# Expert mixture of a two-layer diffusion backbone: experts in pairs, latent rows in two partition halves, context rows in native fp32

## The reference, cut to what matters

```python
D_MODEL, SEQ, CTX_LEN, DEPTH = 1024, 512, 256, 2
N_EXPERTS, EXPERT_FF, CAPACITY_FACTOR = 16, 1024, 2

def _expert_choice_ffn(h, w_router, w1, w3, w2):
    B, T, D = h.shape
    cap = CAPACITY_FACTOR * T // N_EXPERTS
    aff = jax.nn.softmax((h @ w_router).astype(jnp.float32), axis=-1)
    vals, idx = lax.top_k(aff.transpose(0, 2, 1), cap)
    xg = jax.vmap(lambda hb, ib: hb[ib])(h, idx)
    hid = jax.nn.silu(jnp.einsum('becd,edf->becf', xg, w1)) * jnp.einsum('becd,edf->becf', xg, w3)
    y = jnp.einsum('becf,efd->becd', hid, w2) * vals[..., None].astype(h.dtype)
    return jax.vmap(lambda yb, ib: jnp.zeros((T, D), h.dtype).at[ib.reshape(-1)].add(yb.reshape(-1, D)))(y, idx)

# in each layer l: latent stream always, context stream in layer 0 only, with the same weights
ml = _expert_choice_ffn(hl, w_router[l], w_exp_gate[l], w_exp_up[l], w_exp_down[l])
xl = _layer_norm(alpha * xl + g2 * ml, ln2_g[l], ln2_b[l])
```

## Time and profile before

| | |
|---|---|
| median of 3 runs | 3953.68 us (3949.96 to 3955.05) |
| the profiled execution | 3951.19 us, span 3949.5 us |
| busy: PE, weight loads, DVE, ACT, POOL | 3482.3, 2718.0, 2316.6, 1588.2, 779.9 us |
| expert stage of layer 0, of layer 1 | about 1467 to 2168 us, 3255 to 3912 us of the span |
| weight matmuls of the experts (L1228) | 4608 |
| scatter matmuls (L835, 96 rows) | 680 |
| adds to acc (L2042) | 340 |
| mean granted TensorE clock | 0.942 of 2.4 GHz |

### The profile page before, as it was taken

One profiled execution on the slowest core, in us unless ns is written; L12 is line 12 of the kernel. 1 busy time (PEld: TensorE's weight loads), 2 busy tenths in 40 slices (PEclk: granted clock), 3 DMA queues, 4 the chain that ended last, 5 costly groups with the idle time before them and its releaser, 6 DMA issues.

```text
span 3949.5 us, 50430 instructions
## 1 busy us (share of the span) xinstructions
PE 3482.3 (88%) x19426; PEld 2718.0 (69%) x19426; DVE 2316.6 (59%) x3472; ACT 1588.2 (40%) x2055; POOL 779.9 (20%) x467
## 2 busy tenths in 40 slices
PE   5998898889999869999998199898899969999994
PEld 3997677878887746666665189578766756666663
DVE  2594741501111649998997674742322359999996
ACT  3113742411110226666664322754211126666662
POOL 2001013121110113323322200112222112222231
PEclk7999999999999989999998599999999979999997
DMA  6131123031112359888897122131122219999994
GB/s 236 66 128 59 44 97 118 17 107 39 58 64 76 109 184 308 311 309 306 309 311 268 60 75 75 49 97 43 40 94 96 90 61 317 324 327 327 328 331 150
DMA packets 331412, 632.85 MB, mean 160 GB/s; under 512 B 14142, under 2 KB 104398, under 8 KB 324846
## 3 DMA queue, kind: packets, MB, share of 16 engines
q1 hardware_dynamic: 309056, 557.88, 40.7%
q0 software_dynamic: 22192, 72.68, 5.6%
HBM read 614.00 MB, written 16.50 MB: 160 GB/s over the span
## 4 chain that ended last, share of the span: by engine, by line
PE 65%; DVE 11%; issue 9%; ACT 6%; DMA 5%; POOL 2%; POOLq 1%; DVEq 0%; PEld 0%; ACTq 0%; PEldq 0%; SPq 0%
PE ps L835 42%; PE ps L1228 13%; ACT hx L1493 2%; PE ps L953 2%; DVE part L2035 2%; PE ps L985 2%; DMA raw<-in_w_exp_down 1%; DMA raw<-in_w_mod 1%; DMA raw<-in_w_exp_gate 1%; PE ps L971 1%; DVE area L1638 1%; ACT area L1349 1%; POOL hx L782 1%; POOLq L526 1%; PE ps L973 1%
## 5 line engine op out<-in xcount | busy, mean ns | idle before, releaser
L835 PE MATMUL ps<-hx,part 128*128 128x384 f32 (+2 forms) x4704 | 932.8, 357 | 58.9 <-POOLq L526 45.5
L835 PEld LDWEIGHTS ps<-hx,part 128*128 128x128 f32 x4704 | 834.0, 190 | 146.4 <-POOLq L526 46.4
L1228 PE MATMUL ps<-part,hx 128*96 128x512 f32 x3072 | 759.3, 398 | 24.6 <-DVE part L2035 17.5
L2035 DVE TENSOR_TENSOR part<-raw,part 128x2048 fp32r<-128x2048 f32 x256 | 617.1, 2411 | 81.2 <-ACT part L1493 80.7
L1228 PEld LDWEIGHTS ps<-part,hx 128*96 128x96 f32 x3072 | 492.9, 163 | 235.4 <-DVE part L2035 35.6
L1493 ACT ACTIVATE part<-raw 128x2048 fp32r<-128x2048 f32 x256 | 490.0, 1915 | 199.5 <-PE ps L1228 172.6
L512 POOL TENSOR_TENSOR part<-raw,part 128x2048 fp32r<-128x2048 f32 x52 | 237.4, 4567 | 844.5 <-ACT part L509 844.5
L1228 PE MATMUL ps<-hx 128*96 128x512 f32 x1536 | 378.6, 395 | 4.2 <-DVE hx L2035 2.5
L835 PE MATMUL ps<-part,hx 128*128 128x256 f32 (+2 forms) x2208 | 313.8, 304 | 17.3 <-DVEq L526 15.6
L1228 PEld LDWEIGHTS ps<-hx 128*96 128x96 f32 x1536 | 247.6, 162 | 112.7 <-POOL hx L782 5.8
L835 PEld LDWEIGHTS ps<-part,hx 128*128 128x128 f32 x2208 | 293.8, 197 | 34.6 <-DVEq L526 16.1
(11 more groups left out here) (250 smaller groups left out, 3836.2 us busy)
## 6 DMA issues: line engine op xcount, KB each, us to landing
raw<-in_w_exp_gate SPq DMA_DIRECT2D x128, 1024.0 KB, 5.5
raw<-in_w_exp_up SPq DMA_DIRECT2D x128, 1024.0 KB, 5.6
raw<-in_w_exp_down SPq DMA_DIRECT2D x128, 1024.0 KB, 5.7
raw<-in_w_mod SPq DMA_DIRECT2D x48, 1024.0 KB, 7.5
raw<-in_w_in SPq DMA_DIRECT2D x44, 1024.0 KB, 5.6
raw<-in_w_gate SPq DMA_DIRECT2D x32, 1024.0 KB, 6.5
area<-in_bias POOLq DMA_DIRECT2D x32, 512.0 KB, 4.1
raw<-in_w_branch SPq DMA_DIRECT2D x16, 1024.0 KB, 7.3
```

What stands on the lines that cost most here:

```text
L835: last = mm(dst, a, b, start=i == 0, stop=i == len(pairs) - 1)
L1228: last = mm(ps[0:CAP, bank, :], x, y, start=kh == 0 and a == 0, stop=kh == 1 and a == len(pairs) - 1)
L2035: V.tensor_tensor(expert_part(s, 1), src, expert_part(s, 0).bitcast(f32), ALU.subtract).then_inc(S("split_v"), 1)
```

## The change

Two experts share one scatter of their latent rows. The even expert (j = 0) has its 64 latent rows in partitions 0 to 63 and its 32 context rows in 64 to 95; the odd one has context in 0 to 31 and latent in 64 to 127. All token-row tiles get 128 columns, so that each weight matmul, transpose and turned half has 128 columns (of these the unused ones hold leftovers). `put`, `y_hi` and `y_lo` hold the latent rows of both and are scattered once per pair, 128 contraction rows, during the blocks of the next even expert. The context rows have tiles of their own, `y_ctx` and `put_ctx`, kept in plain fp32, and are scattered by one native fp32 matmul per step during the blocks of the odd expert (layer 0 only).

```diff
-def scatters(b, count):
-    double = max(count - 8, 0)
-    first = b + min(b, double)
-    return range(first, first + (2 if b < double else 1)) if b < 8 else range(0)
+def scatters(j, b, per):
+    if j == 0:
+        return range(b, b + 1) if b < 2 * TL else range(0)
+    c = 2 * TL + b // 2
+    return range(c, c + 1) if b % 2 == 0 and c < per else range(0)
...
-        put, o = cut(hx, 0, TOK)
+        y_ctx, o = cut(work, o, D)
+        put_ctx, o = cut(work, o, CTX)
+        put, o = cut(hx, 0, LAT)
         y_hi, y_lo, o = parts_of(hx, o, D)
-        hd_hi, hd_lo, o = parts_of(hx, o, KD, CAP)
-        xg_hi, xg_lo, o = parts_of(hx, o, KD, CAP)
+        hd_hi, hd_lo, o = parts_of(hx, o, KD, P)
+        xg_hi, xg_lo, o = parts_of(hx, o, KD, P)
+        rows_of = [(slice(0, CAPL), slice(CAPL, CAP)), (slice(P - CAPL, P), slice(0, CAPC))]
...
-                        nc.gpsimd.tensor_copy(xg_hi, src).then_inc(*S("xg", l).by(1))
+                        moves = [(rows_of[j][0], src[:, :, 0:CAPL]), (rows_of[j][1], src[:, :, CAPL:CAP])][:2 if full == NT else 1]
+                        for at, x in moves:
+                            last = nc.gpsimd.tensor_copy(xg_hi[:, :, at], x)
...
+                def scatter(c, bank, rows):
+                    half, t = scattered(c)
+                    at = slice(half * NCH, (half + 1) * NCH)
+                    if t < TL:
+                        last = passes(ps[:, bank, :], [(put[rows, t * P:(t + 1) * P], y[rows, at]) for y in (y_hi, y_lo)])
+                    else:
+                        last = mm(ps[:, bank, :], put_ctx[rows, (t - TL) * P:(t - TL + 1) * P], y_ctx[rows, at], start=True, stop=True)
+                    last.then_inc(*S("e_comb", l).by(1))
...
-                                last = mm(ps[0:CAP, bank, :], x, y, start=kh == 0 and a == 0, stop=kh == 1 and a == len(pairs) - 1)
+                                last = mm(ps[:, bank, :], x, y, start=kh == 0 and a == 0, stop=kh == 1 and a == len(pairs) - 1)
...
                             if b == 0:
                                 pe.wait_ge(*S("e_yL", l).at(i * 4 + 2 * j + 2))
-                            for c in scatters(b, ncomb):
-                                scatter(c, i * 2 * ncomb + (ncomb * j + 1))
+                            for c in scatters(j, b, per):
+                                pe.wait_ge(*S("e_acc", l).at(i * per + (c + 1)))
+                                scatter(c, 4, slice(0, P) if c < 2 * TL else slice(0, CAP))
...
-                for c in range(ncomb):
-                    scatter(c, E * ncomb + 1)
+                for c in range(per):
+                    pe.wait_ge(*S("e_acc", l).at(E // 2 * per + 1 + max(c - 3, 0)))
+                    scatter(c, c % 4, slice(0, P) if c < 2 * TL else slice(0, CAPC))
...
-                            act.wait_ge(*S("e_comb", l).at(i * 4 * full + (2 * full * (j + 1) + 1)))
-                            fn(y_hi[0:m, half * NCH:(half + 1) * NCH], ps[0:m, 5 + half, :], ACT.Copy,
-                               scale=val[0:m, 0:1]).then_inc(*S("e_yH", l).by(1))
+                            act.wait_ge(*S("e_comb", l).at(i * per + ((per if j else 2 * TL) + 1)))
+                            for r, y in list(zip(rows_of[j], (y_hi, y_ctx)))[:2 if ctx_out else 1]:
+                                last = fn(y[r, half * NCH:(half + 1) * NCH], ps[r, 5 + half, :], ACT.Copy, scale=val[r, 0:1])
+                            last.then_inc(*S("e_yH", l).by(1))
...
                 for s in range(AHEAD):
                     hi(0, s)
+                for y in (y_hi, y_lo):
+                    for half in range(2):
+                        last = fn(y[:, half * NCH:(half + 1) * NCH], consts[:, 0:NCH], ACT.Copy, scale=0.0)
+                last.then_inc(*S("y_zero", l).by(1))
...
-                if not ctx_out:
-                    V.memset(xgT[:, :, :, CAPL:CAP], 0.0)
```

## The result

| | before | changed |
|---|---|---|
| median of 4 runs each, same chip | 3954.36 us | 3907.98 us |
| lowest to highest | 3949.96 to 3960.37 | 3904.49 to 3910.44 |
| ratio, 95% interval | | 0.988 [0.9864, 0.9895] |
| span of the profiled execution | 3949.5 | 3908.8 |

The account below looks back on a forecast made before the run. TensorE was taken to bound A to B, a chain through ACT and DVE B to A. Gains of 34.8 us in layer 0 and 26.7 in layer 1, together 61.5, from 3951.2, plus 2.5 to the median, gave 3892 us; range 3868 to 3926.

Parts of the forecast that it names:

- The path: Expert turns: a matmul less before B is worth its full time, a DVE add less before B nothing.
- A and B: A: an expert's first scatter matmul, behind block 0; B: first transpose behind block 8. Between them TensorE decides, 27.96 or 26.24 us.
- the forecast stall: TensorE waiting at block 5 for POOL's remainder: 1.55 us in layer 1's odd turns, 0.7 in layer 0's, 0.2 in even turns.
- B to A: Expert's end to the next one's first scatter, 13.87 or 12.78 us; changes only if the chain over ACT and DVE does.
- Fp32 matmuls ... 512 in 0.43: Layer 0's context scatters: 256 fp32 columns stream in 14.06/64 = 0.22 us, so each 512-column matmul costs 0.43 us.
- Rival (c): An fp32 matmul costs twice the 0.43 us: 36 context scatters add 15 us, 3907 us; chance 0.05.
- ACT and DVE otherwise: 160 fewer DVE adds (109 us) and ACT writing `y` in two pieces in layer 0 change nothing in the time.
- the waits for `e_yL` stay: The waits for `e_yL` remain at block 0 of both experts of a pair, with no change in time.
- I take nothing: 128 weight columns for 96 in all 4608 weight matmuls cost nothing; bounds 4 ns gained, 28 ns lost per matmul.
- rival (d): More gain: wide weights bring the gather's spacing (12 us) or POOL's stall is partly absorbed, 3878 us; chance 0.12.
- POOL's token rows ... gain 0.45 per expert: Layer 1's GpSimd copies and subtracts 512 columns, not 768, so block 11's remainder on DVE shortens: 0.45 us per expert.
- Closing scatters: After each layer's last expert, four banks at 0.86 us per scatter: 15.0 us to 11.1 and 7.7, gains 4 and 7.

Follow-up runs that it names:

- `nopool`: Changed kernel with VectorE making every remainder and GpSimd none: 3884.86 us, ratio 0.9837 to the kernel before.
- `addfirst`: Changed kernel with VectorE's addition at block 0 of a turn put ahead of the remainder: 3910.01 us, ratio 0.9887 to the kernel before.
- `w128`: Kernel before with all token-row tiles 128 columns wide instead of 96, scatters as before: 3961.39 us, ratio 1.0037.
- `close4`: Kernel before with only its closing scatters spread over four banks: 3935.86 us, ratio 0.9957.
- `table`: Changed kernel with scatters one block later, VectorE making every remainder, and ScalarE's one-column Silu behind the first high part: 3873.99 us.
- `ylate`: As `table`, with VectorE's subtraction for the first half of y moved from block 10 to block 11: 3873.98 us.
- `early_val`: Changed kernel, scatters one block later, VectorE making every remainder, first y subtraction at block 11, value sums at block 8 not 9: 3898.05 us.

## Why the prediction was right, and where it fell short

- **The path.** Right: a matmul less between A and B is worth its time, a DVE addition less nothing. Odd turns of layer 1 came out at 36.5 as forecast, with the forecast stall; `nopool` gave back 1.55. But B to A, which the sum had 0.3 us longer in layer 0 and 0.25 shorter in layer 1, is 0.5 longer in even turns of both.
- **"Fp32 matmuls ... 512 in 0.43".** Wrong by two: 0.88 us. The step that failed is 14.06/64, since a fp32 matmul is two rows of the trace. For layer 0's 28 in the odd turns that is 12.6 us. Of its 1.8 a turn 0.7 took the place of GpSimd's stall, which the sum had booked beside it, and 0.4 was made up by the spacing of the weight matmuls, so odd periods are 39.77 and not 39.1 (5.5 us over the seven). Rival (c) had the mechanism, with a chance of 0.05, and nearly the time (3907), partly by luck.
- **"ACT and DVE otherwise": nothing, and "the waits for `e_yL` stay".** Wrong in layer 0's even turns. ACT's second write of `y` a half lies, with the table load, on the way to the remainder and the addition behind it, and TensorE's pause before scatter 0 is followed by 3.4 us at the lower clock. Together 1.4 us a turn in five of the seven, 7.8 us in all: an even period is 42.0, and 40.47 where neither shows (`addfirst`). The prediction named the price of this cover ("each piece would cost its own time once per half") but not the clock.
- **"I take nothing" for the 128 columns.** Right for the loads, and the gather's spacing of rival (d) did come: 0.227 a matmul for 0.231, 0.4 us a turn or some 12 us that the sum didn't have. Wrong as a whole: `w128` is 13 us slower, 11 of them in layer 1, with VectorE's remainder at 3.90 us for 2.28.
- **"POOL's token rows ... gain 0.45 per expert".** It did not reach TensorE. At an odd expert's end block 11's remainder is free of GpSimd now (2.29 us for 2.77) and ends 0.26 us earlier, but VectorE's last `y_lo` starts 12.15 us behind B for 11.68. At an even expert's end GpSimd starts first, block 9's remainder takes 3.13 us, and block 10 waits 0.2 for `hd_lo`. Layer 1's even periods are 39.3 to 40.9 for 38.8, 7.3 us over the seven. Most of that is B to A and block 5's wait for GpSimd (0.22 to 0.64 us); without that helper they are 39.05, near the forecast partly by luck, since B to A is still 0.5 longer than before and the spacing makes up for 0.4.
- **Closing scatters.** Better by 5 us: 16.1 for 11 in the change, 16.7 in `close4` alone. They are a third of the change's gain, and have nothing to do with pairing. The 0.86 us a scatter was read at the lower of TensorE's two levels, and most of the shorter stretch ran at the upper one.

Sum: short are 5.5 (odd turns of layer 0), 7.8 (its even turns), 7.3 (even turns of layer 1) and 1.7 (layer 1's last period, 41.2 us for 40.4 before where 0.9 less was forecast). More came in layer 1's odd turns (20.1 us for 17.6, since before had strays there, 39.8 to 40.1), at the layers' ends (5.1) and at the first experts (0.2). That is 14.5 us less than forecast, as in the table. The range held by its width, and by the ends and the spacing, which went the other way. **Open:** who wins between GpSimd and VectorE when they start within 0.1 us, and why the clock drops behind the pause of 1.8 us in five even turns and not in the other two.

## What to carry to other kernels

Before dividing a row's time by its count, find in the code how many instructions those records are: for fp32 matmuls it was two rows each. When a change shortens a full engine's work, price anew the helpers that were harmless: giving VectorE back GpSimd's remainder was worth 7 us before the change and 17 to 23 behind it, and with the scatters a block later the kernel comes to 3867 us. Price a stretch at both levels of the clock where the stalled one that it replaces ran at the lower, and count what an engine's next small instruction stands ahead of: of the four reorderings `addfirst`, `table`, `ylate` and `early_val` none gained, and `table` lost 7 and `early_val` 31 us.

## What the runs showed that was not expected

- Two instructions of the same shapes on GpSimd and VectorE, started 0.08 us apart, took 4.08 and 2.28 us in one kernel and 1.84 and 3.90 in another: one of the two waited until the other had ended.
- 24 scatter matmuls in 6.44 us at a granted clock of 1.00 in four banks; the same 24 took 14.9 us at 0.58 in banks 4 and 7, the last ones in bank 4 alone.
- Moving a one-column Silu behind one copy made two table loads of 1.28 us out of one.
